# A mixture-of-experts kernel on one core: expert weights loaded by pairs of experts, kind by kind, in place of a staggered order

## The reference

```
expert_id, top_w = route(h)          # 1 group of 4, then 2 experts of the group's 8
for each of the 32 experts e:
    y_e = (silu(x_e @ w_gate[e]) * (x_e @ w_up[e])) @ w_down[e]    # x_e: the rows routed to e
out[token] = sum of top_w * y_e over the token's 2 experts
```

## Time and profile before

| | us |
|---|---|
| median of 3 runs (2211.34 to 2218.06) | 2213.01 |
| the profiled execution's own time | 2214.41 |
| its span | 2212.6 |
| TensorE busy (matmul) | 2030.1 (92%) |
| VectorE busy | 1002.7 (45%) |
| ScalarE busy | 681.1 (31%) |
| DMA moved | 619.86 MB, mean 280 GB/s |
| rounds of layer 0's mixture | about 1067 to 1545 of the span |
| rounds of layer 1's mixture | about 1715 to 2194 of the span |

### The profile page before, as it was taken

One profiled execution on the slowest core, in us unless ns is written; L12 is line 12 of the kernel. 1 busy time (PEld: TensorE's weight loads), 2 busy tenths in 40 slices (PEclk: granted clock), 3 DMA queues, 4 the chain that ended last, 5 costly groups with the idle time before them and its releaser, 6 DMA issues.

```text
span 2212.6 us, 29572 instructions
## 1 busy us (share of the span) xinstructions
PE 2030.1 (92%) x9701; PEld 1112.2 (50%) x9702; DVE 1002.7 (45%) x2231; ACT 681.1 (31%) x1085; POOL 45.9 (2%) x79
## 2 busy tenths in 40 slices
PE   8879999999899999999898988898997999889886
PEld 4534777745567776645333333343774344333342
DVE  2273888321568635434443333434324443333334
ACT  1142000011500002142454444444202554444443
POOL 2000000000000000000000000001000000000000
PEclk9869999999899999999899999999999999999998
DMA  8502898434169643413699999998655899999995
GB/s 286 209 1 83 334 350 316 181 141 172 39 240 363 233 168 133 152 39 130 243 423 422 422 413 422 422 422 336 237 191 209 312 422 422 422 422 422 422 422 208
DMA packets 78478, 619.86 MB, mean 280 GB/s; under 512 B 9632, under 2 KB 9952, under 8 KB 15664
## 3 DMA queue, kind: packets, MB, share of 16 engines
q1 hardware_dynamic: 67824, 540.51, 61.1%
q0 software_dynamic: 6912, 66.33, 8.0%
q10 hardware_dynamic: 3648, 11.89, 1.3%
HBM read 605.06 MB, written 13.63 MB: 280 GB/s over the span
## 4 chain that ended last, share of the span: by engine, by line
PE 64%; DMA 26%; DVE 5%; ACT 2%; issue 2%; DVEq 0%; SPq 0%; ACTq 0%
PE ps L838 26%; DMA big<-in_w_up 24%; PE ps L1048 14%; PE ps L1222 11%; PE ps L1060 7%; PE ps L1224 2%; PE ps L852 2%; PE ps L1195 2%; ACT big L1706 1%; DMA big<-in_w_gate 1%; DMA big<-in_dense 0%; DMA big<-in_w_down 0%; DVE x_res L2521 0%; DVE big L2101 0%; PE ps L1206 0%
## 5 line engine op out<-in xcount | busy, mean ns | idle before, releaser
L1222 PE MATMUL ps<-big,hT 128*32 128x512 f32 x3072 | 705.9, 612 | 91.8 <-ACT big L1706 84.3
L1224 PE MATMUL ps<-big,hT 128*32 x1536 | 704.7, 612 | 0.0
L1706 ACT COPY big<-big 128x1024 f32 x384 | 396.1, 1046 | 500.1 <-PE ps L1224 301.9
L2445 DVE TENSOR_SCALAR big<-big 128x1024 f32 x384 | 265.0, 692 | 535.6 <-PE ps L1224 326.4
L1222 PEld LDWEIGHTS ps<-big,hT 128*32 128x32 f32 x3072 | 190.0, 112 | 457.9 <-issue 248.1
L1048 PE MATMUL ps<-hT,big 128*128 128x256 f32 x1408 | 311.1, 379 | 0.0
L838 PE MATMUL ps<-big,hT 128*128 128x512 f32 (+4 forms) x792 | 298.2, 535 | 3.9 <-ACT hT L1647 2.3
L1048 PEld LDWEIGHTS ps<-hT,big 128*128 128x128 f32 x1408 | 266.7, 190 | 49.0 <-issue 14.8
L838 PEld LDWEIGHTS ps<-big,hT 128*128 128x128 f32 x792 | 143.6, 194 | 147.7 <-issue 139.1
L838 PE MATMUL ps<-big 64*30 64x256 f32 (+12 forms) x684 | 156.7, 520 | 27.3 <-issue 5.5
L1224 PEld LDWEIGHTS ps<-big,hT 128*32 128x32 f32 x1536 | 159.1, 112 | 11.5 <-issue 3.7
(11 more groups left out here) (332 smaller groups left out, 1245.6 us busy)
## 6 DMA issues: line engine op xcount, KB each, us to landing
big<-in_w_down SPq DMA_DIRECT2D x128, 1024.0 KB, 22.7
big<-in_w_gate SPq DMA_DIRECT2D x128, 1024.0 KB, 24.3
big<-in_w_up SPq DMA_DIRECT2D x128, 1024.0 KB, 23.4
big<-in_dense SPq DMA_DIRECT2D x52, 1536.0 KB, 8.5
big<-in_dense POOLq DMA_DIRECT2D x28, 2048.0 KB, 10.1
big<-in_dense SPq DMA_DIRECT2D x21, 2048.0 KB, 7.9
y_rows<-c_res ACTq DMA_DIRECT2D x30, 384.0 KB, 7.0
big<-in_dense SPq DMA_DIRECT2D x5, 1024.0 KB, 9.0
```

The costliest lines, as they stand in the source:

```text
L1222: nc.tensor.matmul(ps[g * SLOTS:(g + 1) * SLOTS, bank, :], xT[:, k, g * SLOTS:(g + 1) * SLOTS], side[:, g - 1, quarter % 2, at:at + BW], s ...
L1224: return nc.tensor.matmul(ps[0:SLOTS, bank, :], xT[:, k, 0:SLOTS], experts3[:, bass.ds(here, 1), kind * CH + row:kind * CH + row + BW] .re ...
L1706: nc.scalar.copy(side[:, 1, quarter % 2, :], experts3[:, bass.ds(there, 1), lo:lo + QW] .rearrange("p a n -> p (a n)")).then_inc(s["side2_ ...
L2445: ts(side[:, 0, quarter % 2, :], experts3[:, bass.ds(there, 1), lo:lo + QW].rearrange("p a n -> p (a n)"), 1.0, None, mult).then_inc(s["si ...
```

## The change

Behind g3 on, the loads are issued by pairs of experts. For e = 3, 5, 7, ... 27 `pair` issues g(e), g(e+1), u(e), u(e+1), d(e), d(e+1). Behind the last pair (27, 28) expert 29 is loaded whole (g29, u29, d29), and then the pair 30, 31, kind by kind. The waits of each half are the same as before, only their place in SP's list changes; `need_i` is read once per expert instead of three times. No other engine's program changes.

```diff
--- before.py
+++ after.py
@@ -773,17 +773,19 @@
                                  weights[kind][bass.ds(e + layer * E, 1), :, lo:lo + CH // 2]
                                  .rearrange("a p n -> p (a n)")).then_inc(full[BPE * q + kind], 16)
 
-                def again(e, q, kinds):
-                    quarters = sp.value_load(need_i[0:1, bass.ds(e - BPE, 1)], min_val=2, max_val=12 * ROUNDS)
-                    for kind in kinds:
+                def need(e):
+                    return sp.value_load(need_i[0:1, bass.ds(e - BPE, 1)], min_val=2, max_val=12 * ROUNDS)
+
+                def again(kind, *experts):
+                    for e, q, quarters in experts:
                         for half in range(2):
                             sp.wait_ge(done.sem, quarters + (done.base + 4 * kind + 2 * half))
                             put(kind, e, q, half)
 
-                def staggered(e, q):
-                    again(e, q, (0,))
-                    again(e - 1, (q + BPE - 1) % BPE, (2,))
-                    again(e, q, (1,))
+                def pair(e, q):
+                    a, b = (e, q, need(e)), (e + 1, (q + 1) % BPE, need(e + 1))
+                    for kind in range(3):
+                        again(kind, a, b)
 
                 if layer == 0:
                     for q in range(3 * BPE):
@@ -799,14 +801,18 @@
                     put(kind, 2, 2, 0)
                     put(kind, 2, 2, 1)
                 after(sp, "route" + tag)
-                again(BPE, 0, (0, 1))
-                whole = (E - BPE - 1) // BPE
+                whole = (E - BPE) // (2 * BPE)
                 with sp.Fori(0, whole) as i:
                     for u in range(BPE):
-                        staggered(i * BPE + (BPE + 1 + u), (1 + u) % BPE)
-                for e in range(BPE + 1 + whole * BPE, E):
-                    staggered(e, e % BPE)
-                again(E - 1, (E - 1) % BPE, (2,))
+                        pair(i * (2 * BPE) + (BPE + 2 * u), 2 * u % BPE)
+                rest = BPE + whole * 2 * BPE
+                for e in range(rest, E - 3, 2):
+                    pair(e, e % BPE)
+                a, b, c = ((e, e % BPE, need(e)) for e in range(E - 3, E))
+                for kind in range(3):
+                    again(kind, a)
+                for kind in range(3):
+                    again(kind, b, c)
 
             for q in range(3):
                 sp.sem_inc(slot_full[6 + q], 16)
```

## The result

| | before, us | after, us |
|---|---|---|
| median of 10 runs (lowest to highest) | 2212.89 (2206.68 to 2218.06) | 2224.31 (2219.35 to 2229.32) |
| profiled execution | 2214.41 | 2224.2 |
| its span | 2212.6 | 2222.3 |

The change makes the kernel slower by 11.4 us, half a per cent and clear of the noise, and the two profiled executions differ by 9.8.

The account below looks back on a forecast made before the run. Loads, with DMA full at 422 GB/s, were taken to bound the mixtures from about round 4 on. 0 + 23.1 - 16.3 = +6.8 us: profiled 2221.2, median 2219.8, range 2203 to 2227.

Parts of the forecast that it names:

- Head, 0: Start of each layer: g4 fills the queue's gap in round 0, but g5 lands when it did; 0 us.
- Round 7, +23.1: Layer 0, round 7: u15 and d15 stand behind g16's late release; the layer's rest is 23.1 us later (18.5 to 26).
- the first trip: Layer 0, round 7: first of three successive trips from TensorE's release over the DMA to TensorE's wait, together +23.1 us.
- The ends, -7.1 and -9.2: Rounds 14 and 15: last weights come one or two places earlier; gains 5.2 + 1.9 (layer 0), 2.6 + 6.6 (layer 1).
- no wait for DMA in rounds 14 and 15: Sign for both layers' last two rounds; a wait for DMA in round 15 would refute the ends' gain.
- Middle of layer 1, nothing: Layer 1 has no place like layer 0's round 7, so the new list costs nothing there.
- g16's wait doesn't start the trips: Faster rival, layer 0 round 7: only the queue's gap of 5.6 us is paid; -11 us, 2202; chance 0.14.
- the ends gain nothing: Slower rival, last rounds: waits for round 13 hold up g30 and g31; +23 us, 2236; chance 0.08.
- the head's 4.97 count in each layer as a gain of their own: No-change rival: head's gain cancels layer 0's least cost; +2 less a part of 9.9, 2205 to 2215; chance 0.12.
- the fixed part: A lone half's issue to landing: 4.8 us in the trace; the skill's 4.4, three trips 1.2 shorter, not used.

Follow-up runs that it names:

- e7: Kernel before with a new start (g3 g4 u3 u4 d3 g5 d4 u5) and end (g29 u29 d28 d29, then 30, 31 by kind): 2204.29 us, 0.9952 of before.
- e8: Kernel before with only the end changed, behind u28: g29 u29 d28 d29, then g30 g31 u30 u31 d30 d31: 2214.7 us in one run.
- e10: Kernel after, but in both layers the pair 3, 4 by kind, experts 5 to 29 whole, then the pair 30, 31: 2216.18 us, 1.0019 of before.
- e4: Kernel after, but in layer 1 expert 16's loads wait for releases one round later than needed: 2248.07 us in one run.
- e2: Kernel after, but in layer 0 expert 15 is loaded whole, then expert 16 whole: 2202.67 us, 0.9951 of before.
- e1: Kernel after, but layer 0 keeps the old staggered order and only layer 1 has the new one: 2203.86 us, 0.9961 of before.
- e9: Kernel after, but layer 0 goes g15 u15 d15 g16 u16 g17 u17 d16 d17 g18 u18 d18, then pairs from 19: 2196.8 us, 0.9931 of before.
- e6: Kernel before with only the start changed to g3 g4 u3 u4 d3 g5 d4 u5: 2206.11 us, 0.9964 of before.
- e3: Kernel after, but in layer 0 the pair 15, 16 goes g15 u15 g16 u16 d15 d16: 2211.88 us in one run.
- e5: Kernel after, but the pairs run through (29 with 30) and expert 31 is loaded alone at the end: 2230.98 us in one run.

## Why the prediction was right

The prediction was slower by 6.8 us of a profiled execution, at 2219.8 in the median, with a range of 2203 to 2227; measured were 2224.31, and 10.5 in the layers. The median alone would not show that the working was right, since two terms of some 23 and 16 us stand against each other in it; so each is held against the trace. Its steps, one by one:

- **Head, 0.** Right for the head's own rounds. g5's first half went at 1102.33, as before (1102.04), and rounds 1 to 6 differ by -1.3 and +0.2.
- **Round 7, +23.1.** The mechanism is right in each link, the size is 2.5 to 3.2 short. The links, in us of the span:

| | predicted | measured |
|---|---|---|
| g16's second half goes | 1277.2 | 1278.9 |
| u15's first half lands | 1284.5 | 1286.5 |
| up 1, up 2 | 1291.9, 1295.3 | 1294.4, 1297.9 |
| d15's first half lands | 1302.7 | 1305.3 |
| down 1, down 2 | 1311.4, 1316.0 | 1313.1, 1317.7 |
| g19's first half lands | 1353.1 | 1356.8 |

 g19 landed at 1330.5 before, so it is 26.3 later, and rounds 7 and 8 together take 92.2 in place of 66.6, +25.6. This is the term that was mis-sized. Of it 1.7 come before the first trip: the "gate releases of round 7" were taken over from before, but TensorE worked off the gate part at a granted clock of 0.68 (window from 1270) where it had 1.00; it had come to the gate part a little earlier and had waited 2.7 us for g15, 1.6 before. The response from u15's landing to up 1 was 7.9 for 7.4, and that from d15's landing to down 1 7.8 for 8.7; together they cancel. Another 2.0 lie between d16's second half (1322.6) and g19: 34.2 and not 13 x 2.48 = 32.2. Of these 0.7 are the queue's restart: SP first had to issue g17 behind d16 (1319.56), it landed 3.2 later and not 2.48, and the window from 1320 shows 400 GB/s. Some 0.9 more are the store of round 7's result, which the count of halves left out: its 384 KB went at 1333.01 and landed at 1341.31, and 0.39 MB / 422 GB/s are 0.93 us. The last 0.4 is not traced.
- **The ends, -7.1 and -9.2.** Right, by row, with 6.7 and 8.8 measured. Layer 0: round 14 -5.0 (predicted 5.2), round 15 -1.7 (1.9). Layer 1: -2.6 (2.6) and -6.2 (6.6). SP's rows of round 14 are now, in layer 0:

```profile
1513.57 8.62 SPq L772 DMA_DIRECT2D big<-in_w_gate  x4
...
1529.51 12.17 SPq L772 DMA_DIRECT2D big<-in_w_down  x4
```

 Gate 2 is at 1513.57 + 8.62 - 0.33 = 1521.86, down 2 at 1529.51 + 12.17 - 0.33 = 1541.35 and down 1 4.64 ahead of it (4.97 - 0.33), at 1536.71. From gate 2 to down 1 it takes 14.85 us where it took 19.9, and 14.7 unhindered. What the prediction did not say is how the gain comes about: it counted places behind g29, "with d28 already brought", and this missing d28 is the lead of round 0. That the head is worth 0 is right for its own rounds, but the ends' gain rests on the head's gap filled, at the other end of the list (e7, e8, e10).

 One sign named in advance did not come clean: no wait for DMA in rounds 14 and 15. The chain of the kernel after has two in layer 0, for g29 at the start of round 14 and for d31 in round 15:

```profile
1486.81 26.24 DMA big<-in_w_gate
...
1536.71 17.87 DMA big<-in_w_down
```

 Before, round 14 began with the same wait (its gate part is 8.7 long in both, 6.9 unhindered), so it takes nothing off the gain. The second costs about the 0.4 us named above; the prediction would have had such a wait refute the term, but by its size it doesn't.
- **Middle of layer 1, nothing.** Right: rounds 1 to 13 differ by 0.3 us (e4 shows what one late slot would have cost).
- **Rivals.** That g16's wait doesn't start the trips is excluded by the windows. e2, which brings u15 and d15 in time as this rival supposed, came to 2202.67 where the rival's price was 2202. That the ends gain nothing is excluded by e1. That the head's 4.97 count in each layer as a gain of their own is excluded by rounds 1 to 6.

The chance given to slower, 0.41, was as large as that of no change, since the sum stood at the edge of what can be measured. With the 2.5 to 3.2 of round 7 in the sum, 9 to 10 us, it would have stood clear of it.

On the fixed part: the section of the Trainium skill that the prediction used (DMA: Bandwidth & Descriptors, section on the anatomy of one DMA) gives its 2.0 us plus bytes / 436e3 for DMAs of the gpsimd path, and the loads here are issued by SP, so the estimate of 4.4 us carried it over to another path. With no load ahead of it u16's first half took 4.9 us from issue to landing and d16's 5.1; g16's took 6.0, beside a store of 384 KB that went at 1275.40. Each is longer than the estimate. That a semaphore wait happens on the issuing sequencer, as the same section says, the trace shows: in the row of 36.31 us above SP issues nothing from 1246.64 to 1275.43, g16's release.

## What to carry to other kernels

In a list of loads in one queue with waits in it, an entry is as late as the latest wait ahead of it. Before reordering such a list, write the release that each entry waits for beside it, with its time from the trace; an entry whose release lies a round later than its neighbours' should stand behind everything that this round itself still needs (e2), and behind what else is free to go (e9). And where DMA is full, count the bytes that stand ahead of the last use: in this kernel an order gained only by filling a gap, once, and the gain was cashed in at the other end of the list (e6 to e8, e10).

## What the runs showed that I had not expected

- TensorE came back slow from these waits. The products' mean duration in the 60 us of round 7, after and before:

```profile
L1228 PE MATMUL ps<-big,hT 128*32 128x512 f32 x100 | 28.3, 722 | 13.5 <-ACT big L1712 13.4
```
```profile
L1222 PE MATMUL ps<-big,hT 128*32 128x512 f32 x170 | 39.8, 615 | 10.9 <-ACT big L1706 10.5 <-DVE hT L2483 0.4
```

 722 ns for 615. The windows from 1285 and 1305 show a granted clock of 0.50, the lower of the two levels (1.2 GHz), both behind windows in which TensorE had been busy for 0.00 and 1.45 of 5 us. A late release thus also makes the next one later. Layer 1's copy of the pattern (e4) began at full clock (1.00 in the windows from 1925 to 1945), with a gate part of 8.7 in place of 13.1, and cost 24.2 where rounds 7 and 8 of layer 0 lost 25.6.

 It also makes an early arrival cost time. In layer 0 of before, e1, e2 and e3 TensorE waited 1.5 to 1.6 us for g15, and round 7's gate part took 10.2 to 10.5 us; of after, e4, e5, e8 and e9 it came earlier, waited 2.7 to 3.3, and the gate part took 13.1 to 14.5. Counted from g15's landing the gate part ended after 8.7 to 8.9 us in the first group and 10.4 to 11.4 in the second.
- A single round is a poor witness. e8 has the order of before up to u28, and yet its rounds 1 to 6 in layer 0 took 166.8 (before 168.4) and its rounds 7 and 8 69.1 (66.6): TensorE came earlier to a load that lands at its own time, waited longer (3.3 us for g15, 1.6 before) and came back slower (a granted clock of 0.50 in the window from 1268 to 1273, 1.00 before). Sums over a stretch that ends at a wait for DMA repeat better (layer 1's rounds 1 to 13 in after, e1 and e9: 391.1, 391.2 and 391.3).
